# Projection matmuls of a hybrid decoder block issued in steps of three through the FoX, SSD and GLA stages, and the SSD convolution in two overlapping phases

## The chip, the cores and the metric

The kernel runs on one core of a Trainium2 chip. The metric is the device time of one execution in microseconds (us), lower is better. Engine names as in the profile: PE is TensorE (PEld its weight loads), DVE is VectorE, ACT is ScalarE, POOL is GpSimd, SP is SyncE, which here only issues DMAs.

## What is computed

One decoder layer over 1024 tokens of width 1024, batch 1, float32:

```
h = rms_norm(x);  p = h @ W_in          # 3352 columns, cut among four head groups
x += W_out @ concat[ FoX attention | Mamba-2 SSD | GLA | HGRN2 ]   # 256 wide each
x += cross_attention(rms_norm(x), rms_norm(mem))                   # 256 memory tokens
x += conv_glu_ffn(rms_norm(x))                                     # 2816 wide
```

FoX is causal softmax attention with 4 heads of 64 and a forget bias. SSD runs a causal convolution of width 4 with a SiLU over 512 channels, then a chunked scan in 8 chunks of 128 tokens. GLA and HGRN2 are chunked gated linear attentions. The memory's keys and values are `rms_norm(mem) @ xa_wkv`.

## The kernel before

**Projections.** Every large product is made of float32 numbers split in a high and a low part, so one 128-row contraction costs three matmuls (`split_matmuls`, lines 99 to 101). The input projection is cut in 27 items of 128 columns. An item has two halves of 512 tokens, and a half is 8 contraction blocks, thus 24 matmuls of 128x512 into one of two PSUM buffers (`mix_gb`). Here three matmuls of one contraction block are called a step: a half is 8 steps. For each item ACT writes the high part of the weights (line 432), DVE the low part (line 739), and ACT copies each finished half out of PSUM (line 444). The half m needs the low part of its item (semaphore `g_lo`) and half m-2 copied out (`g_ev`). After the input projection, 16 further items (`kv`) multiply the memory's rows with `xa_wkv`; each of them is 4 steps. SP loads each item two items ahead.

**Stages and order.** Each engine's program is written out by hand, stage after stage: normalise x, project; HGRN2; preparation of FoX; FoX; SSD; GLA; then another block (`tail_block`) with W_out, cross attention and feed-forward. While a stage's own work keeps DVE and ACT busy, TensorE is given projection work of the stage after it. How many halves go where is a table of counts that `spread` turns into ranges; all engines walk the same table, each doing its share of a half at that place:

```
_FX = spread(2 * S0, 2 * G0, [1] * 6 + [1 if n in (4, 9, 14, 20, 25, 30) else 0 for n in range(33)])
_SD = spread(2 * G0, 2 * N_ITEMS, [2, 2, 1, 1] + [1] * 6 + [0] * 2)
```

- Preparation of FoX: six rounds. In each, PE does two norm matmuls (line 1074), one half of projection, and transposes of v (line 1180); ACT squares (484), takes Ln (491) and Exp (493), and copies v; DVE multiplies (750). Then ACT and DVE gate HGRN2's output (tanh line 537; DVE 754, 755), and only then DVE begins FoX's logits (875).
- FoX: 33 bodies, 32 units (head pair, block of 128 queries, head). Body n on PE: scores of unit n+1 (1205), projection if the table has any (6 bodies), then `outputs(n-1)`: transposes of the probabilities (1219), a wait for ACT's copy of them (617), and their product with v (1227). DVE makes logits and probabilities (875 to 885), ACT the exponentials (606).
- SSD: the convolution takes 4 tiles of 128 channels. For each tile ACT starts with scale and bias (646), DVE adds three taps (908 twice, 910), ACT takes Tanh (649), DVE forms the product (913). PE does 6 halves meanwhile. Then 8 chunks: PE does a half (chunks 0 to 5), the inputs of the next chunk (1256, 1261, 1266), then the outputs (1292, 1294, 1297). A chunk's outputs wait for DVE's and ACT's work on the chunk, which waits for the outputs of the chunk before. ACT's memory statistics (467 to 472) and DVE's scaling (962) come in chunk 5, the transposes of the memory (1280) in chunks 6 and 7.
- Preparation of GLA: gates, norms of SSD's output, and a chain of exponentials and products (987 to 1009), with the `kv` items 0 to 10 on PE. Then 8 GLA tiles (1317 to 1349) with no projection, then items 11 to 15 among the last norms.

Of the kernel before, what the change touches and what calls it, by code (L numbers as in the profile page):

```python
# [156 lines left out]
FOX_PRE, FOX_UNIT = _FX[:6], _FX[6:]  # L157
_SD = spread(2 * G0, 2 * N_ITEMS, [2, 2, 1, 1] + [1] * 6 + [0] * 2)
SSD_CONV, SSD_CHUNK = _SD[:4], _SD[4:]


KV_ITEMS = 4 * KT // 2


MEM_STATS, MEM_TR = NT - 3, NT - 2


def mixers_block(nc, cst, a, SL, MX, HH, HL, x, FCW, FCB):
# [4 lines left out]
    with Phase(nc, "mix") as ph:  # L173
# [248 lines left out]
        def _(act):  # L422
# [156 lines left out]
            for j in range(6):  # L579
                rstd(2 * j)  # L580
                rstd(2 * j + 1)
                if j < 5:
                    squares(2 * j + 2)
                    squares(2 * j + 3)
                halves(*FOX_PRE[j])
# [36 lines left out]
            for n in range(len(FOX_UNITS) + 1):  # L622
# [8 lines left out]
                halves(*FOX_UNIT[n])  # L631
                fox_out(n - 1)
            copy_out(2 * G0)
# [6 lines left out]
            for t in range(4):  # L640
                halves(*SSD_CONV[t])
# [3 lines left out]
                y, th = mx(4 + t % 2), data(B + 6 + t % 2)  # L645
                act.activation(y, data(B + 2 + t), ACT.Identity, scale=CWS[:, t, 3:4], bias=CBS[:, t:t + 1])\
                   .then_inc(E("conv_in"), 1)
                act.wait_ge(E("conv_sum"), t + 1)
                act.activation(th, y, ACT.Tanh).then_inc(E("conv_th"), 1)
            for c in range(NT):  # L650
                halves(*SSD_CHUNK[c])
                if c == MEM_TR:
                    copy_out(2 * N_ITEMS)
# [4 lines left out]
                act.activation(EA, M[2][:], ACT.Exp).then_inc(E("s_ea"), 1)  # L658
                if c == MEM_STATS:
                    memory_stats()  # L660
                if c >= MEM_TR:
                    memory_hi(c - MEM_TR)

            act.wait_ge(E("s_upd"), NT)
            act.wait_ge(E("s_yev"), NT)
            kv(0, 1)
            for p in range(2):
                gate(2 + p, data(B + p), data(B + 6 + p))
            kv(1, 2)
# [8 lines left out]
            kv(2, 4)  # L678
            rstd(18)
            rstd(19)  # L680
            kv(4, 6)
# [5 lines left out]
            kv(6, 7)  # L687
            act.wait_ge(E("gl_cum"), 1)
            act.activation(data(B + 6), data(B + 7), ACT.Exp, scale=1.0 / 16).then_inc(E("gl_e1"), 1)
            kv(7, 8)  # L690
            act.wait_ge(E("gla_q"), 1)
            act.activation(data(B + 6), data(B + 7), ACT.Exp, scale=-1.0 / 16).then_inc(E("gl_e2"), 1)
            kv(8, 9)
            act.wait_ge(E("gl_te"), 1)
            act.activation(data(B + 7), data(B + 7), ACT.Exp, scale=1.0 / 16).then_inc(E("gl_e3"), 1)
            kv(9, 11)
# [9 lines left out]
            kv(11, 12)  # L706
# [9 lines left out]
            kv(12, 14)  # L716
            rstd(22)
            rstd(23)
            kv(14, 15)
# [7 lines left out]
        def _(dve):  # L727
# [126 lines left out]
            for j in range(6):  # L854
                norms(2 * j, 2 * j + 2)
                halves(*FOX_PRE[j])
# [30 lines left out]
            for n in range(33):  # L887
# [3 lines left out]
                halves(*FOX_UNIT[n])  # L891
                if n:
                    probabilities(n - 1)
                if n in (0, 16):
# [7 lines left out]
            for t in range(4):  # L902
                s = B + 2 + t
                y, th = mx(4 + t % 2), data(B + 6 + t % 2)
                halves(*SSD_CONV[t])
                dve.wait_ge(E("conv_in"), t + 1)
                for j in (2, 1):
# [3 lines left out]
                   .then_inc(E("conv_sum"), 1)  # L911
                dve.wait_ge(E("conv_th"), t + 1)
                dve.scalar_tensor_tensor(data(s), th, 1.0, y, ALU.add, ALU.mult).then_inc(E("conv_out"), 1)
            dve.wait_ge(E("conv_out"), 4)
            S = S_SSD
            for c in range(NT):
                sd = SCD[c % 2]
                halves(*SSD_CHUNK[c])
# [37 lines left out]
                dve.nop().then_inc(E("s_upd"), 1)  # L956
                if c == MEM_STATS:
# [7 lines left out]
                if c >= MEM_TR:  # L965
# [6 lines left out]
            kv(0, 1)  # L972
            gate(2, data(B), data(B + 6), mx(2))
            kv(1, 2)
            gate(3, data(B + 1), data(B + 7), mx(3))
            norms(16, 18)
            kv(2, 4)
# [3 lines left out]
            kv(4, 6)  # L981
# [12 lines left out]
            kv(6, 7)  # L994
# [4 lines left out]
            kv(7, 8)  # L999
# [7 lines left out]
            kv(8, 9)  # L1007
            dve.wait_ge(E("gl_e3"), 1)
            dve.tensor_tensor(k, k, u, ALU.mult).then_inc(E("gl_kend"), 1)
            kv(9, 11)  # L1010
# [20 lines left out]
            kv(11, 12)  # L1031
            norms(20, 22)
            kv(12, 14)
            norms(22, 24)
            kv(14, 15)
# [5 lines left out]
        def _(pe):  # L1041
            def halves(m0, m1):
                for m in range(m0, m1):
                    n, h = half_at(m)
                    if h == 0:
                        pe.wait_ge(E("g_lo"), n + 1)
                    if m >= 2:
                        pe.wait_ge(E("g_ev"), m - 1)
                    for k in range(KT):
                        mm = split_matmuls(pe, gb[m % 2][:], WH[:, n % PART, k, :], WL[:, n % PART, k, :],  # L1050
                                           half(HH[:, k, :], h), half(HL[:, k, :], h), k == 0, k == KT - 1)
                    mm.then_inc(E("g_mm"), 1)

            def kv(j0, j1):
                for j in range(j0, j1):
                    n, (c, kk) = N_ITEMS + j, divmod(j, KT // 2)
                    pe.wait_ge(E("g_lo"), n + 1)
                    if kk == 0:
                        pe.wait_ge(E("g_ev"), 2 * (N_ITEMS + c))
                    for t in range(2):  # L1060
                        tok = slice(t * P, (t + 1) * P)
                        for b in range(2):
                            k = 2 * kk + b
                            mm = split_matmuls(pe, gb[t][:], HH[:, k, tok], HL[:, k, tok], two_rows(WH, n % PART)[:, b, :],
# [1158 lines left out]
```

## Time and profile before

| what | value |
|---|---|
| median of 3 executions | 1868.43 us |
| the three executions | 1868.43, 2946.23, 1867.78 us |
| the profiled execution | 1867.99 us |
| its span in the trace | 1866.2 us |
| TensorE busy in the span | 1731.4 us (93%) |
| mean granted TensorE clock | 0.966 of full speed |

The span is what the trace covers; 1.8 us of the profiled execution lie outside it. Busy times of TensorE are modelled from pipelined matmuls and overlap one another, so the spacing of the starts is what a matmul costs.

### The profile page before, as it was taken

To read this page: it belongs to the slowest core of one execution; us is meant where nothing else is said; L and a number is where in the kernel's file an instruction comes from. 1 tells how busy PE (TensorE), PEld (TensorE's weight loads), DVE (VectorE), ACT (ScalarE), POOL (GpSimd) and SP (SyncE) were. 2 spreads that over 40 slices of the span, in tenths; PEclk is the share of its full clock that TensorE was granted. 3 is DMA by queue.
4 is the path that set the end of the run, shared out by engine and by line. 5 is a ranking of instruction groups with operands and counts; after the bars stand their busy time and mean duration, and the time that the engine had idled before them with its cause. 6 is when DMAs were issued, how large, how long until landed. Compare 5 with 4: busy or idle time off the path is not lost.

```text
span 1866.2 us, 20863 instructions
## 1 busy us (share of the span) xinstructions
PE 1731.4 (93%) x8076; PEld 1374.7 (74%) x8076; DVE 889.6 (48%) x1487; ACT 676.2 (36%) x1218; POOL 74.2 (4%) x119
## 2 busy tenths in 40 slices
PE   6999998988888769699999999999999999999997
PEld 5787665655567546587888888888888888888886
DVE  4315584453636656545334434555543355555332
ACT  5224103633452353634434322434432334344321
POOL 2000430000001002000000000000000000000000
PEclk8999998898999899899999999999999999999999
DMA  4122000000002021350001102333323333433232
GB/s 138 45 47 46 13 12 12 23 12 12 12 23 68 12 68 57 111 194 11 14 1 46 45 29 87 94 102 91 96 74 96 101 113 98 123 92 107 85 96 96
DMA packets 166922, 121.32 MB, mean 65 GB/s; under 512 B 23448, under 2 KB 140456, under 8 KB 166824
## 3 DMA queue, kind: packets, MB, share of 16 engines
q1 hardware_dynamic: 165496, 115.53, 20.8%
q10 hardware_dynamic: 1328, 4.46, 0.7%
q8 instruction: 65, 1.06, 0.2%
q14 instruction: 33, 0.27, 0.0%
HBM read 115.77 MB, written 4.19 MB: 64 GB/s over the span
## 4 chain that ended last, share of the span: by engine, by line
PE 57%; DVE 1%; ACT 0%; DMA 0%; issue 0%; DVEq 0%
PE tail_b L99 17%; PE tail_b L101 17%; PE tail_b L100 17%; PE tail_b L2065 2%; PE tail_b L2040 1%; PE tail_b L2029 0%; PE tail_b L2052 0%; PE tail_b L1977 0%; DVE tail_wl L1741 0%; DMA tail_wr<-in_w_out 0%; PE tail_b L2184 0%; PE tail_b L2100 0%; DVE tail_xs L1776 0%; ACT tail_xs L1576 0%; DVE XR L1904 0%
## 5 line engine op out<-in xcount | busy, mean ns | idle before, releaser
L1897 DVE TENSOR_TENSOR ff_wl<-ff_wr,ff_wh 128x512 fp32r<-128x512 f32 (+1 forms) x176 | 168.5, 958 | 329.9 <-ACT ff_wh L1684 329.9
L1684 ACT ACTIVATE ff_wh<-ff_wr 128x512 fp32r<-128x512 f32 (+1 forms) x176 | 148.7, 846 | 377.9 <-PE tail_b L101 377.9
L99 PE MATMUL tail_b<-HH,ff_wh 128*128 128x512 f32 x704 | 273.9, 389 | 0.0
L100 PE MATMUL tail_b<-HL,ff_wh 128*128 128x512 f32 x704 | 273.9, 389 | 0.0
L101 PE MATMUL tail_b<-HH,ff_wl 128*128 128x512 f32 x704 | 273.9, 389 | 0.0
L99 PE MATMUL mix_gb<-HH,mix_wh 128*128 128x512 f32 x432 | 178.3, 413 | 7.7 <-ACT slots L444 3.8
L100 PE MATMUL mix_gb<-HL,mix_wh 128*128 128x512 f32 x432 | 171.5, 397 | 0.0
L101 PE MATMUL mix_gb<-HH,mix_wl 128*128 128x512 f32 x432 | 170.8, 395 | 0.0
L99 PE MATMUL tail_b<-tail_wh,HH 128*128 128x512 f32 x384 | 153.9, 401 | 10.0 <-DVE tail_wl L1741 8.8
L100 PEld LDWEIGHTS tail_b<-HL,ff_wh 128*128 128x128 f32 x704 | 132.2, 188 | 27.7
L99 PEld LDWEIGHTS tail_b<-HH,ff_wh 128*128 128x128 f32 x704 | 132.2, 188 | 27.5
L101 PEld LDWEIGHTS tail_b<-HH,ff_wl 128*128 128x128 f32 x704 | 132.2, 188 | 27.1
L101 PE MATMUL tail_b<-tail_wh,HL 128*128 128x512 f32 x384 | 150.3, 391 | 0.0
L100 PE MATMUL tail_b<-tail_wl,HH 128*128 128x512 f32 x384 | 150.2, 391 | 0.0
L739 DVE TENSOR_TENSOR mix_wl<-mix_wr,mix_wh 128x1024 fp32r<-128x1024 f32 x43 | 53.6, 1247 | 113.9 <-ACT mix_wh L432 113.3
L99 PEld LDWEIGHTS mix_gb<-HH,mix_wh 128*128 128x128 f32 x432 | 83.5, 193 | 32.5 <-ACT slots L444 5.3
L99 PE MATMUL tail_b<-ff_wh,ff_aha 128*128 128x512 f32 x256 | 100.2, 392 | 0.0
L100 PE MATMUL tail_b<-ff_wl,ff_aha 128*128 128x512 f32 x256 | 99.7, 389 | 0.0
L100 PEld LDWEIGHTS mix_gb<-HL,mix_wh 128*128 128x128 f32 x432 | 83.4, 193 | 18.6 <-issue 1.7
L101 PEld LDWEIGHTS mix_gb<-HH,mix_wl 128*128 128x128 f32 x432 | 83.0, 192 | 17.9
L99 PEld LDWEIGHTS tail_b<-tail_wh,HH 128*128 128x128 f32 x384 | 72.6, 189 | 24.8 <-issue 11.0
L101 PEld LDWEIGHTS tail_b<-tail_wh,HL 128*128 128x128 f32 x384 | 72.4, 188 | 15.6
(311 smaller groups left out, 2661.7 us busy)
## 6 DMA issues: line engine op xcount, KB each, us to landing
ff_wr<-in_ffn_w_up SPq DMA_DIRECT2D x88, 512.0 KB, 3.7
ff_wr<-in_ffn_w_down SPq DMA_DIRECT2D x88, 256.0 KB, 2.8
mix_wr<-in_w_in SPq DMA_DIRECT2D x26, 512.0 KB, 3.7
mix_wr<-in_xa_wkv SPq DMA_DIRECT2D x16, 512.0 KB, 3.7
XR<-in_x SPq DMA_DIRECT2D x8, 512.0 KB, 6.4
tail_wr<-in_w_out SPq DMA_DIRECT2D x16, 256.0 KB, 5.2
XR<-in_x ACTq DMA_DIRECT2D x1, 4096.0 KB, 18.7
tail_wr<-in_xa_wq SPq DMA_DIRECT2D x16, 256.0 KB, 4.6
```

The lines of the kernel that those rows point to most:

```text
L99: pe.matmul(out, hi_w, hi_x, start=first, stop=False)
L100: pe.matmul(out, hi_w, lo_x, start=False, stop=False)
L101: return pe.matmul(out, lo_w, hi_x, start=False, stop=last)
L739: dve.tensor_tensor(WL[:, n % PART, :, :], WR[:, n % RAW, :, :], WH[:, n % PART, :, :], ALU.subtract)\
L1684: act.activation(part(FWH[m % FPART], m), part(FWR[m % FRAW], m), ACT.Copy).then_inc(w_hi, 1)
L1897: dve.tensor_tensor(part(FWL[m % FPART], m), part(FWR[m % FRAW], m), part(FWH[m % FPART], m), ALU.subtract)\
L2040: mm = pe.matmul(bank[3 + g][:, hh * N_MEM:(hh + 1) * N_MEM], QT[:, 2 * h + kk, :], ktr(2 * h + kk), start=(kk == 0), stop=(kk == 1))
L2065: mm = pe.matmul(bank3[6 + g][:, j, :], vv(m, d), PT[:, m, d // 2, :], start=(m == 0), stop=(m == 1))
```

## The change

No instruction of PE is added or taken away. The tables now count steps, and TensorE's `fill` issues a range of steps, which may begin or end inside a half. The other engines do their share of a half in the body in which it begins (`begun`). The steps go as follows (before in brackets):

- FoX preparation: 2 steps in each of 6 rounds (8).
- FoX: in bodies 1 to 31 except 16, 2 steps between the scores and the transposes (part A) and, unless n is a multiple of 4, one more between the transposes and the product with v (part B). Together 84 steps (48).
- SSD convolution: 9 steps for each of 4 tiles, 36 in all (48). On ACT the bias of two tiles is set first, and on DVE the taps of tile t+1 come ahead of the product of tile t.
- SSD chunks: 6 steps before and 6 after the next chunk's inputs, in chunks 0 to 4, 60 in all (48 in chunks 0 to 5). The memory's statistics come in chunk 4 and its transposes in chunks 5 and 6. The first `kv` item (4 steps) goes ahead of the outputs of chunk 7.
- GLA: 24 `kv` steps in the preparation (44), one step at each of two places in each of 8 tiles (0), then 4, 8 and 8 (the same).

```diff
+def FOX_FILL(n):
+    return (0, 0) if n in (0, 16) else (2, 1 if n % 4 else 0) if n < 32 else (0, 0)
...
-_FX = spread(2 * S0, 2 * G0, [1] * 6 + [1 if n in (4, 9, 14, 20, 25, 30) else 0 for n in range(33)])
-_SD = spread(2 * G0, 2 * N_ITEMS, [2, 2, 1, 1] + [1] * 6 + [0] * 2)
+def begun(span):
+    return -(-span[0] // KT), -(-span[1] // KT)
+_FX = spread(2 * S0 * KT, 2 * G0 * KT, [2] * 6 + [c for n in range(33) for c in FOX_FILL(n)])
+_SD = spread(2 * G0 * KT, 2 * N_ITEMS * KT, [9] * 4 + [c for n in range(NT) for c in ((6, 6) if n < 5 else (0, 0))])
+_KV = spread(0, KV_ITEMS * KV_STEPS, [4] + [4, 4, 4, 4, 4, 4] + [c for n in range(NT) for c in (1, 1)] + [4, 8, 8])
-MEM_STATS, MEM_TR = NT - 3, NT - 2
+MEM_STATS, MEM_TR = NT - 4, NT - 3
...
 # ACT, FoX body
-                halves(*FOX_UNIT[n])
                 fox_out(n - 1)
+                halves(*begun((FOX_A[n][0], FOX_B[n][1])))
...
 # ACT, convolution
+            conv_bias(0)
+            conv_bias(1)
+            for t in range(4):
+                halves(*begun(SSD_CONV[t]))
+                conv_tanh(t)
+                if t + 2 < 4:
+                    conv_bias(t + 2)
...
 # DVE, convolution
+            conv_taps(0)
+            for t in range(4):
+                halves(*begun(SSD_CONV[t]))
+                if t + 1 < 4:
+                    conv_taps(t + 1)
+                conv_gate(t)
...
 # PE
+            def fill(s0, s1):
+                for s in range(s0, s1):
+                    m, k = divmod(s, KT)
+                    n, h = half_at(m)
+                    if k == 0 and h == 0:
+                        pe.wait_ge(E("g_lo"), n + 1)
+                    if k == 0 and m >= 2:
+                        pe.wait_ge(E("g_ev"), m - 1)
+                    mm = split_matmuls(...)
+                    if k == KT - 1:
+                        mm.then_inc(E("g_mm"), 1)
...
-                halves(*FOX_UNIT[n])
-                outputs(n - 1)
+                fill(*FOX_A[n])
+                outputs(n - 1, FOX_B[n])
...
 # PE, SSD chunk c
-                halves(*SSD_CHUNK[c])
+                fill(*SSD_A[c])
...
                     ssd_inputs(c + 1)
+                fill(*SSD_B[c])
+                if c == NT - 1:
+                    pe.wait_ge(E("mem_lo"), 4)
+                    kv(*KV_SSD)
...
 # PE, GLA tile i
                 gla_states(i)
+                kv(*KV_A[i])
                 if i + 1 < NT:
                     gla_scores(i + 1)
+                kv(*KV_B[i])
                 gla_outputs(i)
```

TensorE in FoX, first half of the heads, around the unit with four blocks of keys, before (L1205 scores, L1219 transposes, L1227 product with v):

```order
L1205 MATMUL mix_m<-XR 128x512
L1205 MATMUL mix_m<-XR 128x128
L1219 MATMUL mix_m<-ident,slots 128x128 x4
L1227 MATMUL mix_m<-mix_scratch,slots 64x128 x4
L1205 MATMUL mix_m<-XR 128x512
```

and in the changed kernel, where L1251, L1265 and L1274 are those three lines:

```order
L1251 MATMUL mix_m<-XR 128x512
L1251 MATMUL mix_m<-XR 128x128
L99 MATMUL mix_gb<-HH,mix_wh 128x512
L100 MATMUL mix_gb<-HL,mix_wh 128x512
L101 MATMUL mix_gb<-HH,mix_wl 128x512
L99 MATMUL mix_gb<-HH,mix_wh 128x512
L100 MATMUL mix_gb<-HL,mix_wh 128x512
L101 MATMUL mix_gb<-HH,mix_wl 128x512
L1265 MATMUL mix_m<-ident,slots 128x128 x4
L99 MATMUL mix_gb<-HH,mix_wh 128x512
L100 MATMUL mix_gb<-HL,mix_wh 128x512
L101 MATMUL mix_gb<-HH,mix_wl 128x512
```

The row L1274 follows. Two steps now stand ahead of the transposes and one behind them; before, this body had none.

ACT at the start of the SSD convolution, before (L432 weights, L444 copy out, L646 bias, L649 Tanh):

```order
L432 ACTIVATE mix_wh<-mix_wr 128x1024
L444 ACTIVATE slots<-mix_gb 128x512
L646 ACTIVATE XR<-slots,mix_cbs,mix_cws 128x1024
L649 ACT_TABLE_LOAD
L649 ACTIVATE slots<-XR 128x1024
L444 ACTIVATE slots<-mix_gb 128x512
```

and in the changed kernel (L456, L468, L670 and L675 in the same roles):

```order
L670 ACTIVATE XR<-slots,mix_cbs,mix_cws 128x1024 x2
L456 ACTIVATE mix_wh<-mix_wr 128x1024
L468 ACTIVATE slots<-mix_gb 128x512
L675 ACT_TABLE_LOAD
L675 ACTIVATE slots<-XR 128x1024
L670 ACTIVATE XR<-slots,mix_cbs,mix_cws 128x1024
```

The bias of the first tile no longer stands behind a copy that waits for TensorE's first half.

## Rows read from the trace of the kernel before

**Rows 1.** The page: the span, and TensorE's granted clock in 40 slices.
```profile
span 1866.2 us, 20863 instructions
...
PEclk8999998898999899899999999999999999999999
```

**Rows 2.** Busy per stage: stretch, length, PE, PEld, DVE, ACT, POOL, granted clock, DMA share, GB/s.
```profile
307.10:357.60 50.50, 50.46 (x192) 35.22 (x192) 16.85 (x19) 33.87 (x57) 0.00 (x0) 0.96 0.12 32
357.60:437.60 80.00, 67.76 (x337) 45.67 (x336) 43.19 (x91) 32.12 (x77) 0.00 (x0) 0.94 0.05 14
...
533.80:572.90 39.10, 32.96 (x145) 26.97 (x145) 23.91 (x19) 16.99 (x19) 0.52 (x1) 0.97 0.16 41
572.90:631.40 58.50, 57.15 (x343) 46.89 (x343) 34.33 (x83) 14.89 (x25) 5.85 (x16) 0.96 0.16 55
631.40:658.40 27.00, 14.33 (x70) 9.53 (x69) 17.13 (x41) 6.65 (x15) 0.00 (x0) 0.68 0.00 1
658.40:713.30 54.90, 39.03 (x142) 28.15 (x141) 34.08 (x33) 29.11 (x35) 2.91 (x2) 0.91 0.29 95
713.30:746.70 33.40, 32.24 (x202) 19.28 (x200) 20.22 (x42) 7.55 (x16) 8.70 (x7) 0.97 0.06 18
```

**Rows 3.** Timeline ahead of FoX: start, length, engine, line, operation, last wait in brackets.
```profile
324.37 1.88 PE L1074 MATMUL mix_m<-slots,mix_bo 128*128 128x512 f32 x4
...
325.43 0.69 ACT L491 ACTIVATE slots<-mix_m,eps 128x512 f32<-128x512 f32 x1 [0.42 <-PE mix_m L1074]
...
327.92 1.14 ACT L484 ACTIVATE slots<-XR 128x512 f32<-128x512 f32 x2
...
347.90 0.69 ACT L491 ACTIVATE slots<-mix_m,eps 128x512 f32<-128x512 f32 x1 [2.12 <-PE mix_m L1074]
...
358.58 0.35 DVE L875 SCALAR_TENSOR_TENSOR slots<-mix_m,mix_st,slots 128x128 f32<-128x128 f32 x1 [0.32 <-PE mix_m L1205]
```

**Rows 4.** TensorE's timeline, one FoX body near 415 us.
```profile
411.69 0.87 PE L1219 MATMUL mix_m<-ident,slots 128*128 128x128 f32 x6
413.12 1.50 PE L1227 MATMUL mix_m<-mix_scratch,slots 128*64 128x128 f32 x12 [0.56 <-ACT mix_scratch L617]
...
416.46 0.77 PE L1219 MATMUL mix_m<-ident,slots 128*128 128x128 f32 x5
```

**Rows 5.** TensorE's timeline, projection matmuls in FoX body 20.
```profile
456.77 0.63 PE L99 MATMUL mix_gb<-HH,mix_wh 128*128 128x512 f32 x1
457.20 0.63 PE L100 MATMUL mix_gb<-HL,mix_wh 128*128 128x512 f32 x1
...
457.92 0.40 PE L99 MATMUL mix_gb<-HH,mix_wh 128*128 128x512 f32 x1
...
460.68 0.39 PE L99 MATMUL mix_gb<-HH,mix_wh 128*128 128x512 f32 x1
```

**Rows 6.** Timeline, third tile of the SSD convolution.
```profile
559.89 2.60 DVE L908 SCALAR_TENSOR_TENSOR XR<-slots,mix_cws,XR 128x1024 f32<-128x1024 f32 x2
...
563.84 1.06 ACT L649 ACTIVATE slots<-XR 128x1024 f32<-128x1024 f32 x1 [3.99 <-DVE XR L910]
...
564.93 1.22 DVE L913 SCALAR_TENSOR_TENSOR slots<-slots,XR 128x1024 f32<-128x1024 f32 x1 [1.13 <-ACT slots L649]
```

**Rows 7.** TensorE's timeline, first output matmuls of SSD chunks 5, 6 and 7.
```profile
629.91 0.45 PE L1292 MATMUL mix_m<-XR,slots 128*64 128x128 f32 x4
...
642.16 0.70 PE L1292 MATMUL mix_m<-XR,slots 128*64 128x128 f32 x4
...
652.51 0.70 PE L1292 MATMUL mix_m<-XR,slots 128*64 128x128 f32 x4 [3.73 <-DVE XR L937]
```

**Rows 8.** Timeline from the SSD norms to the first GLA tile.
```profile
680.24 0.69 ACT L491 ACTIVATE slots<-mix_m,eps 128x512 f32<-128x512 f32 x1 [4.13 <-PE mix_m L1074]
...
689.28 0.74 DVE L987 TENSOR_SCALAR slots<-mix_m,mix_bg 128x512 f32<-128x512 f32 x1
...
713.30 0.49 PE L1317 MATMUL mix_m<-ident,slots 128*128 128x128 f32 x3
```

More of the change, by code:

```diff
@@ L584, in _ @@
                     squares(2 * j + 3)
-                halves(*FOX_PRE[j])
+                halves(*begun(FOX_PRE[j]))
                 for i in (2 * j, 2 * j + 1):
@@ L639, in _, with conv_bias @@
             act.wait_ge(E("mixed"), 2)
-            for t in range(4):
-                halves(*SSD_CONV[t])
+            conv_y = lambda t: mx(4 + t % 2)
+            def conv_bias(t):
                 act.wait_ge(E("half_w"), 1)
@@ L855, in _ @@
                 norms(2 * j, 2 * j + 2)
-                halves(*FOX_PRE[j])
+                halves(*begun(FOX_PRE[j]))
             for p in range(2):
@@ L890, in _ @@
                     logits(n)
-                halves(*FOX_UNIT[n])
                 if n:
                     probabilities(n - 1)
+                halves(*begun((FOX_A[n][0], FOX_B[n][1])))
                 if n in (0, 16):
@@ L899, in _, with conv_taps @@
             dve.nop().then_inc(E("mixed"), 1)
[L902 to L905, printed above, removed]
+            def conv_taps(t):
+                s, y = B + 2 + t, mx(4 + t % 2)
                 dve.wait_ge(E("conv_in"), t + 1)
@@ L917, in _ @@
                 sd = SCD[c % 2]
-                halves(*SSD_CHUNK[c])
                 dve.wait_ge(E("s_tr"), c + 1)
@@ L956, in _ @@
                 dve.nop().then_inc(E("s_upd"), 1)
+                halves(*begun((SSD_A[c][0], SSD_B[c][1])))
                 if c == MEM_STATS:
@@ L1054, in kv @@
[L1054 to L1064, printed above, removed]
-                                               two_rows(WL, n % PART)[:, b, :], k == 0, k == KT - 1)
+            def fill(s0, s1):
[6 more added lines that the diff above has]
+                        pe.wait_ge(E("g_ev"), m - 1)
+                    mm = split_matmuls(pe, gb[m % 2][:], WH[:, n % PART, k, :], WL[:, n % PART, k, :],
+                                       half(HH[:, k, :], h), half(HL[:, k, :], h), k == 0, k == KT - 1)
+                    if k == KT - 1:
+                        mm.then_inc(E("g_mm"), 1)
@@ new lines, in halves, with kv @@
+            def halves(m0, m1):
+                fill(KT * m0, KT * m1)
+            def kv(u0, u1):
+                for u in range(u0, u1):
+                    j, (t, b) = u // KV_STEPS, divmod(u % KV_STEPS, 2)
+                    n, (c, kk) = N_ITEMS + j, divmod(j, KT // 2)
+                    k, tok = 2 * kk + b, slice(t * P, (t + 1) * P)
+                    if t == 0 and b == 0:
+                        pe.wait_ge(E("g_lo"), n + 1)
+                        if kk == 0:
+                            pe.wait_ge(E("g_ev"), 2 * (N_ITEMS + c))
+                    mm = split_matmuls(pe, gb[t][:], HH[:, k, tok], HL[:, k, tok], two_rows(WH, n % PART)[:, b, :],
+                                       two_rows(WL, n % PART)[:, b, :], k == 0, k == KT - 1)
+                    if b == 1:
@@ L1172, in _ @@
                 norms(2 * j, 2 * j + 2)
-                halves(*FOX_PRE[j])
+                fill(*FOX_PRE[j])
                 for i in (2 * j, 2 * j + 1):
@@ L1206, in scores, with outputs @@
                               start=True, stop=True).then_inc(E("sc_mm"), 1)
-            def outputs(n):
+            def outputs(n, between):
                 hp, i, hh = FOX_UNITS[n]
@@ L1220, in outputs @@
                     last.then_inc(E("p_tr"), 1)
+                fill(*between)
                 if n >= 1:
@@ L1242, in _ @@
                     scores(n + 1)
-                halves(*FOX_UNIT[n])
-                outputs(n - 1)
+                fill(*FOX_A[n])
+                outputs(n - 1, FOX_B[n])
             norms(12, 16)
@@ L1249, in _ @@
             for t in range(4):
-                halves(*SSD_CONV[t])
+                fill(*SSD_CONV[t])
             pe.wait_ge(E("conv_out"), 4)
@@ L1300, in _ @@
                 pe.matmul(M[h][:], WG2[:], half(data(SMALL), h), start=True, stop=True).then_inc(E("gate_mm"), 1)
-            pe.wait_ge(E("mem_lo"), 4)
-            kv(0, 2)
+            kv(*KV_PREP[0])
             norms(16, 18)
-            kv(2, 4)
+            kv(*KV_PREP[1])
             norms(18, 20)
-            kv(4, 6)
-            kv(6, 11)
+            for part in KV_PREP[2:]:
+                kv(*part)
             pe.wait_ge(E("gl_kin"), 1)
```

91 lines of the change are left out of this document (45 added, 46 removed).

## The prediction

> **What bounds the kernel now.** I read the page first. TensorE is the engine to fill: its granted clock is near full almost everywhere, and the slices that are not lie in the first half of the span [rows 1]. So the question is by stage, and the busy time by stretch comes next [rows 2]. From 307 to 747 us TensorE's modelled busy time leaves gaps: 12.2 us of 80.0 in the first half of FoX, 12.7 of 27.0 in SSD's last chunks, 15.9 of 54.9 ahead of GLA. In the preparation of FoX (50.5 us) and in SSD chunks 0 to 5 (58.5 us) it is nearly full. No work is added or removed, so the change can gain only what TensorE now waits, and it moves work from places that are full to places that wait. The timeline tells the price of a step. Its starts are 0.23 us apart at full clock (12 matmuls from 457.92 to 460.68) and 0.43 us at the low one [rows 5]: a step of three costs 0.69 us, a half 5.5 us.
>
> The time is worked out as a walk down TensorE's program, stage by stage, each term measured from the end of the stage before it.
>
> **Preparation of FoX.** Four steps of every eight, and two more, leave each round, 36 in all, or 24.8 us of work. What is late next is ACT. A round now takes 7.49 us (the first Ln of round 3 is at 325.43, that of the sixth at 347.90, three rounds). ACT's two pairs of Ln and Exp take 2.49 (325.43 to 327.92), the next square 0.57 (half of 1.14), about 0.1 until the norm matmul starts, and its Ln follows 1.06 after that (324.37 to 325.43) [rows 3]. That is a loop of 4.2 us, while TensorE has 1.7 of norms, 0.4 of transposes and 1.4 of steps, 3.5 us. I take 4.25 us. The first round, which keeps its weight conversion, saves 2.9; four more save 3.25 each, 13.0. One copy out of PSUM (0.6) leaves ACT's way between the last Exp and the tanh of the gates. DVE's gates then still end last before the first logits at 358.58 [rows 3]. Term: -16.5 us.
>
> **FoX bodies.** 84 steps instead of 48. Part B goes where TensorE waits for ACT's copy: six transposes start at 411.69 and the product with v at 413.12; at 0.11 us each (twelve matmuls of that width last 1.50) the transposes are over at 412.34, so 0.78 us are a wait [rows 4]. A step there costs 0.69 and about 0.14 for the turn from it, so 0.05 us net; up to 0.26 where a unit has seven blocks of keys, nothing where it has four. I take 0.8 us per half of the heads for the nine B steps in bodies 5 to 15. Part A has no wait to hide in once a unit has four blocks: a body of 4.77 us (411.69 to 416.46) is work of TensorE [rows 4], and two steps cost 1.38 and a turn, 1.5 us. In the first bodies of a half it is hidden in part: there the transposes wait for DVE, and matmuls run at 0.43 [rows 5].
> Per half: taken out, three halves of 5.5 and 0.15 (one of them partly at the low clock, 1.6 us more), 18.6 us. Put in, eleven bodies with A at 1.5 (16.5), B 0.8, bodies 1 to 4 together 2.4: 19.7. Term for both: +2.1 us, for 24.8 us of work taken on. If no B step were hidden, 24 of them would add 16 us more; that is the upper bound of this term. If A hid as well, it would be some 10 us less; that is the lower.
>
> **SSD convolution.** It takes 39.1 us [rows 2], of which 48 steps are 33. The DVE rows give its own chain: three taps 3.95 us (559.89 to 563.84), tanh 1.09, product 1.22 [rows 6]. Now the first bias doesn't wait for half 42, and a tile's tanh runs beside the next one's taps. Followed through: taps of tile 0 end 5.2 us after the start, weights' low part 6.4, taps 1 at 10.3, product 0 at 11.6. Then a loop stays: bias 2 waits for product 0, and the ACT part of the next item comes before tanh 1, so taps 2 start at 15.7 and end at 19.6; product 1 at 20.9, bias and taps 3 at 26.0, product 2, the last low part and product 3 at 29.8 us. TensorE is done with 36 steps at 24.8, so DVE ends last. Term: 29.8 instead of 39.0, -9.2 us.
>
> **SSD chunks with steps.** A chunk has 12 steps (8.2 us) and 3.6 us of its own work and turns, 11.8; 8 steps took 8.8 to 9.9. From the first chunk's steps to the first output matmul of the last chunk that has steps it was 54.1 us, six chunks (it is 629.91 there [rows 7]); five chunks now give 4 times 11.75, 10.3 up to the outputs, and 0.6 for one wait for low weights in chunk 2: 57.9. What waits is less than before, since ten microseconds of TensorE's work cover the 7 to 8 of DVE and ACT. Term: +3.8 us.
>
> **SSD chunks without.** Here the change gives back. Chunks without steps are bound by the chain through DVE and ACT: 12.25 us with the memory's scaling (629.91 to 642.16) and 10.35 with its low part (to 652.51), at a clock of 0.68 [rows 2, 7]. Before there were two of them, now three: 12.25, 10.35 and 10.35. Besides, ACT's statistics now stand behind the copy of half 53, which TensorE finishes just before its outputs; DVE waits 1.4 us for them. The `kv` item in chunk 7 (2.7 us) hides in this wait. Term: 34.35 instead of 22.6, +11.8 us.
>
> **GLA.** From the outputs of chunk 7 (652.51) to the first tile it is 60.8 us now (713.30 [rows 7, 8]). With 24 steps instead of 44 the chain of ACT and DVE is bare. The second pair of norms waits for two items (Ln at 680.24); with one it comes at 673.4, and DVE's first GLA operation, now at 689.28 behind two low parts [rows 8], at 677. From there the chain is the same to the last product (at 696), and the seventh item ends at about 697.9. Term: -15.4 us. The tiles are TensorE's: 32.2 of 33.4 us busy [rows 2]. Sixteen steps put in add 11.0, their turns 2, one wait for the copies of `gb` 0.8; the last tile hides 1.8. Term: +12.0 us.
>
> **The sum.** -16.5 + 2.1 - 9.2 + 3.8 + 11.8 - 15.4 + 12.0 = -11.4 us. Against the profiled execution of 1867.99 us (a span of 1866.2 [rows 1] and 1.8 outside it) that is 1856.6; the median of the runs shown is 0.4 higher. I forecast 1857 us, 0.6% less, and so no change that a measurement of this kernel, which tells about 2%, can be sure to see.
>
> **Rival 1: full clock and better hiding (1846 us).** The low stretches of the clock cost matmuls double [rows 5], and steps in nearly every FoX body leave TensorE no long wait. If the clock then stays full at the start of both halves and in the chunks without steps (3 us), and part A hides where I charge it 1.5 us, in a third of 22 bodies (8 us), it is 11 us less. For it: the small bodies at 0.43 us per matmul. Against it: in large bodies TensorE has no wait ahead of the transposes.
>
> **Rival 2: the spread costs what it hides (1866 us).** Steps are begun and ended inside halves, so copies out and low weights can be late in a body. If each of the ten step places of the SSD chunks and every fourth of 54 in FoX loses 0.4 us (4 + 5 us), the gain is 2. For it: ACT now does its share after the exponentials of the chunk. Against it: by the walk above, a copy is two bodies early in FoX.
>
> **Rival 3, slower: TensorE thinned out until its clock drops (1874 us).** In the preparation of FoX it now has 3.5 us of work in 4.25, in that of GLA 24 steps in 45 us. Behind the small units of FoX the trace shows matmuls 0.43 us apart instead of 0.23, the lower of the two levels, 1.2 instead of 2.4 GHz [rows 5], and in SSD's bare chunks a mean of 0.68 of the clock [rows 2]. If it falls in the preparation, a round's work is 7 us instead of 3.5 and passes ACT's 4.25; the round is back near 7.3. It decides from the round in which TensorE's work passes 4.25 us. Price: of the 15.9 us 13 are lost, 2 in the first bodies, and 2 ahead of GLA: +17, 1874. Against it: between 380 and 440 us waits of 0.8 us in each body leave nearly the whole clock (0.94 over that half of FoX with its start [rows 2]).
> The Trainium skill's page "TensorE: Matmul & The Clock Gate", section "What's actually happening", states that the slow clock is the default state and that only activity lifts it, which speaks against spreading work thinly. By that rule the outcome is this rival's 1874 us if the thinned rounds lose the clock, and 1857 us if they keep it; no row here shows rounds of this kind.
>
> **How the numbers follow.** Forecast 0.5 (1851 to 1864 of its own), rival 1 0.22, rival 2 0.16, rival 3 0.12. Bounds: the FoX term reaches from -10 to +16 around its value, the SSD terms some 6 either way, and these seldom agree. A range of 1834 to 1873 leaves out the far part of rival 1 and most of rival 3. Faster by over 2% (below 1831) needs more than rival 1's gain twice over: 0.06. Slower by over 2% needs 37 us: 0.01. Within 2%: 0.93.
>
> **What would show it.** In the profile after: ACT's Ln (L515) in the preparation 4.25 us apart and the first logits near 342; a step between transposes and product (L1265, L1274) with no wait behind it; the convolution 30 us; three SSD output groups over 10 us apart, not two; the first GLA tile 45 us after chunk 7's outputs and tiles of 5.3 us. It would be wrong if rounds stay at 7 us, if bodies with part A grow by less than 1 us, or if the bare chunks take under 9 us.

## The result, and the profile after

The changed kernel takes 1882.97 us (median of 20 executions, 1881.44 to 1891.2), the kernel before 1868.5 us (20 executions, one of them 2946 us and left out of the ratio). The ratio is 1.0078, 95% interval 1.0062 to 1.0094. So the change costs 14.5 us (11.6 to 17.6), under 1% but clear of the spread, where 11 us less was forecast; 1883 lies outside the range of 1834 to 1873. The profiled execution took 1890.98 us, 8 us over the median. Of that, 4.7 us are in HGRN2's stage, ahead of everything that the change touches, at a granted clock of 0.70 in a stretch where the kernel before had 0.93; the stages below are therefore each counted from the end of the one before.

The page of the changed kernel, to be laid beside [rows 1]:

```profile
span 1889.0 us, 20864 instructions
...
PEclk8999988899999888999999999999999999999999
```

The instructions are the same in number but for one. After the first slice the clock is under 0.9 in slices 6 to 8 (236 to 378 us) and 14 to 16 (614 to 756 us), before in 7, 8, 10, 14 and 17 [rows 1]; most of FoX lies between them, so the page alone doesn't place the loss. The windows by stage, columns as in [rows 2] (stretch, length, PE, PEld, DVE, ACT, POOL, granted clock, DMA share, GB/s):

```profile
311.80:345.00 33.20, 28.02 (x84) 15.33 (x84) 13.54 (x16) 29.19 (x51) 0.00 (x0) 0.92 0.06 17
345.00:444.60 99.60, 85.02 (x391) 57.09 (x390) 44.97 (x93) 34.39 (x80) 0.00 (x0) 0.90 0.06 16
444.60:538.20 93.60, 85.52 (x398) 56.44 (x398) 42.42 (x90) 35.29 (x83) 0.00 (x0) 0.95 0.05 12
538.20:579.10 40.90, 31.15 (x120) 21.84 (x118) 26.27 (x23) 24.43 (x31) 0.52 (x1) 0.96 0.10 27
579.10:648.00 68.90, 62.91 (x331) 50.31 (x331) 28.73 (x67) 12.15 (x20) 4.96 (x16) 0.95 0.16 54
648.00:684.00 36.00, 22.32 (x117) 16.13 (x117) 20.90 (x48) 10.91 (x19) 0.00 (x0) 0.72 0.00 0
684.00:726.40 42.40, 26.66 (x100) 18.32 (x97) 30.85 (x35) 23.96 (x29) 1.99 (x2) 0.84 0.22 74
726.40:771.40 45.00, 44.09 (x248) 28.12 (x247) 24.32 (x46) 12.47 (x22) 8.67 (x7) 0.96 0.18 60
```

They are, in order: preparation of FoX, FoX's first and second half, convolution (with the norms ahead of it), SSD chunks with steps, chunks without, preparation of GLA, GLA tiles. FoX takes 193.2 us. The same count made of each trace by the first and last matmuls of the stages gives this account; the predicted terms stand beside it.

| stage | before, us | after, us | difference | predicted |
|---|---|---|---|---|
| preparation of FoX | 50.5 | 33.2 | -17.3 | -16.5 |
| FoX | 164.4 | 193.2 | **+28.8** | +2.1 |
| convolution, with norms | 50.8 | 40.8 | -10.0 | -9.2 |
| SSD chunks | 79.6 | 104.5 | **+24.9** | +15.6 |
| preparation of GLA | 60.8 | 42.8 | -18.0 | -15.4 |
| GLA tiles | 33.2 | 45.1 | +11.9 | +12.0 |
| after them, to the first transposes of the next block | 92.4 | 90.2 | -2.2 | 0 |

The sum is +18.1, and 4.7 ahead of the first row make up the 22.8 us by which the two spans differ. Two terms failed. For FoX the waits are asked first, on DVE, in 345 to 540 us (waiting line, releaser: us in total, times, longest), and below it the same wait in the kernel before, in 357 to 522 us:

```profile
DVE mix_wl L773 <- ACT mix_wh L456: 40.5, 5, 10.1
```
```profile
DVE mix_wl L739 <- ACT mix_wh L432: 9.8, 3, 3.6
```

DVE writes the low part of an item's weights (line 773) from the high part that ACT writes (line 456). It waits up to 10.1 us for it, five times in FoX; before, up to 3.6 us, three times. Two things moved: on ACT the share of the projection went behind the outputs (line 644), as the diff of the change shows, and on DVE, which that diff leaves out, from ahead of the probabilities to behind them. The timeline of the changed kernel around the third of the five waits (start, length, engine, line, operation, idle time and releaser):

```profile
427.30 1.74 PE L1274 MATMUL mix_m<-mix_scratch,slots 128*64 128x128 f32 x14
...
429.07 0.27 ACT L644 ACTIVATE XR<-mix_m 64x128 f32<-64x128 f32 x1 [1.73 <-PE mix_m L1274]
...
429.37 0.60 ACT L468 ACTIVATE slots<-mix_gb 128x512 f32<-128x512 f32 x1
...
429.86 1.05 ACT L456 ACTIVATE mix_wh<-mix_wr 128x1024 fp32r<-128x1024 f32 x1
...
430.95 1.22 DVE L773 TENSOR_TENSOR mix_wl<-mix_wr,mix_wh 128x1024 fp32r<-128x1024 f32 x1 [10.12 <-ACT mix_wh L456]
432.09 1.40 DVE L909 SCALAR_TENSOR_TENSOR slots<-mix_m,mix_st,slots 128x512 f32<-128x512 f32 x2
...
435.18 0.75 DVE L919 TENSOR_SCALAR slots<-slots,mix_rin 128x1024 f32<-128x1024 f32 x1
435.98 1.57 PEld L1265 LDWEIGHTS mix_m<-ident,slots 128*128 128x128 f32 x8 [5.79 <-DVE slots L919]
435.99 1.97 PE L1265 MATMUL mix_m<-ident,slots 128*128 128x128 f32 x8 [5.36 <-DVE slots L919]
...
437.61 0.78 PE L99 MATMUL mix_gb<-HH,mix_wh 128*128 128x512 f32 x1
437.99 0.60 ACT L641 ACTIVATE mix_scratch<-mix_m 128x512 f32<-128x512 f32 x1 [0.26 <-PE mix_m L1265]
438.18 0.63 PE L100 MATMUL mix_gb<-HL,mix_wh 128*128 128x512 f32 x1
...
438.61 0.63 PE L101 MATMUL mix_gb<-HH,mix_wl 128*128 128x512 f32 x1
```

Read it upwards from TensorE's 5.36 us. Its transposes wait for DVE's probabilities (919). These wait behind DVE's logits (909) of the next unit, which start at 432.09, right behind the low part. The low part stood ready in DVE's program for 10.1 us and waited for ACT's 456. ACT's 456 and the copy 468 stand in ACT's program behind line 644, which scales and writes out the unit before, and 644 waits for TensorE's product (1274). So DVE, which is normally a body or two ahead of TensorE, is held until TensorE has finished the body before; its lead is gone, and TensorE pays. Behind the wait matmuls start 0.57 and 0.43 us apart (437.61, 438.18, 438.61), where at full clock it is 0.23 [rows 5]. TensorE's own waits in 345 to 540 us add up to this, and those of the kernel before in 357 to 522 us to what stands in the second block:

```profile
PE mix_m L1265 <- DVE slots L919: 12.4, 5, 5.4
PE mix_m L1251 <- DVE slots L909: 5.6, 2, 2.8
PE mix_m L1274 <- ACT mix_scratch L641: 4.5, 8, 0.8
```
```profile
PE mix_m L1227 <- ACT mix_scratch L617: 19.8, 32, 1.3
PE mix_m L1219 <- DVE slots L885: 4.4, 2, 2.4
```

The waits for DVE are 18.0 us over five items; before, they were 4.4 us, two times. The waits for ACT's copy fell from 19.8 to 4.5 us, as part B was meant to do. So 15.3 us of waits went and 13.6 us of others came: in sum the 36 further steps were hardly hidden.

### The profile page after: what moved, and what is told of

It reads as the page before. It is cut to its first block, busy times and chain, and to the rows that moved or that the text cites. A ratio compares the mean times of both kernels' runs of the same rounds, so it can differ in the third digit from the quotient of the medians.

```text
span 1889.0 us, 20864 instructions
## 1 busy us (share of the span) xinstructions
PE 1747.8 (93%) x8076; PEld 1380.4 (73%) x8076; DVE 887.8 (47%) x1487; ACT 675.2 (36%) x1218; POOL 72.4 (4%) x119
## 4 chain that ended last, share of the span: by engine, by line
PE 56%; DVE 1%; ACT 0%; DMA 0%; issue 0%; DVEq 0%
PE tail_b L99 17%; PE tail_b L101 17%; PE tail_b L100 17%; PE tail_b L2115 2%; PE tail_b L2090 1%; PE tail_b L2079 0%; PE tail_b L2102 0%; PE tail_b L2027 0%; DVE tail_wl L1791 0%; DMA tail_wr<-in_w_out 0%; PE tail_b L2150 0%; PE tail_b L2234 0%; DVE tail_xs L1826 0%; ACT tail_xs L1626 0%; DVE XR L1954 0%
## 5 line engine op out<-in xcount | busy, mean ns | idle before, releaser
L99 PE MATMUL mix_gb<-HH,mix_wh 128*128 128x512 f32 x432 | 186.1, 431 | 7.9 <-ACT slots L468 4.0
L101 PEld LDWEIGHTS tail_b<-tail_wh,HL 128*128 128x128 f32 x384 | 72.5, 189 | 15.6
```

Source lines behind the costliest of these rows:

```text
L99: pe.matmul(out, hi_w, hi_x, start=first, stop=False)
L101: return pe.matmul(out, lo_w, hi_x, start=False, stop=last)
```

## The experiments

Ten runs, each timed beside the kernel before. All but the seventh are edits of the changed kernel. In diffs, `share(n)` stands for `halves(*begun((FOX_A[n][0], FOX_B[n][1])))`, ACT's or DVE's part of the projection in body n.

**1. The share where it stood before.**

```diff
 ACT   fox_exp(n)
-      fox_out(n - 1)
       share(n)
+      fox_out(n - 1)
 DVE   logits(n)
+      share(n)
       probabilities(n - 1)
-      share(n)
```

> The changed kernel, with ACT's and DVE's share of a half (copy out, high part, low part) back at its old place in each FoX body: on ACT ahead of the copies of the unit's outputs, on DVE between logits and probabilities. Theory A (in the changed kernel this share stands behind the outputs, so DVE's next logits wait for a low part that waits for a high part that waits for TensorE's outputs; some 3 to 6 us at each of 6 items, and a low clock after it): the stall is cut but not gone, since the copy now waits for a half that ended only in part A of the same body, and the probabilities stand behind it, about 3 us per item. FoX, 193 us in the changed kernel and 164 before, comes to 180 to 186, the time to 1870 to 1877. Rival B (steps in small pieces cost turns and clock, wherever the share stands): FoX stays at 190 to 193, the time at 1880 to 1883.

Measured: 1882.17 us, ratio 1.0049 (1.0020 to 1.0078); FoX 188.5 us. Only 4.7 us of FoX came back, less than theory A said and more than rival B: this run alone decides nothing. TensorE's waits for the probabilities are no less than in the changed kernel (12.4 us):

```profile
PE mix_m L1265 <- DVE slots L919: 13.3, 7, 2.9
```

The share is now ahead of the outputs on ACT, but on DVE it sits ahead of probabilities that TensorE needs next. The copy that theory A blamed is a small part: in FoX, ACT waited 6.2 us in all for a half to end. Experiment 9 differs from this run in DVE's place alone and takes 165.2 us in FoX, so DVE's place is the cause here.

**2. The share a body later on both engines.**

```diff
 ACT   fox_exp(n)
+      share(n - 1)
       fox_out(n - 1)
-      share(n)
 DVE   logits(n)
+      if n and n != 16: share(n - 1)
       probabilities(n - 1)
-      share(n)
```

> As e1_fox_share_first, but the share of a half that begins in body n is done in body n+1, where the half before it has long ended. Theory A: no engine waits for it any more; FoX comes to the 166 to 169 us of the prediction's walk and the time to 1857 to 1862, the first that is below the kernel before. Rival B: FoX 190 us and 1880 or more.

Measured: 1869.87 us, ratio 0.9999 (0.9966 to 1.0033); FoX 178.3 us, both well above what was expected (1857 to 1862, and 166 to 169). 14.9 of the 28.8 us are back, with no change to TensorE's own program. That the companion engines' order is a cause was now shown; that it was the whole of it was not. The trace still had TensorE waiting for line 919 seven times, up to 3.7 us and 13.0 in all, since on DVE the share again stood ahead of the probabilities.

**3. No steps between transposes and product (part B).** On top of experiment 2:

```diff
-    return (0, 0) if n in (0, 16) else (2, 1 if n % 4 else 0) if n < 32 else (0, 0)
+    return (0, 0) if n in (0, 16) else (3 if n % 4 else 2, 0) if n < 32 else (0, 0)
```

> e2_fox_share_later with the 24 steps of part B moved ahead of the transposes, into part A (3, 0 in place of 2, 1). If the step between transposes and product hides in the wait for ACT's copy, as the prediction has it, it loses 24 times 0.6 to 0.7 us: 14 to 17 us more than e2, 1872 to 1876. If TensorE pays for a step there as elsewhere, it is within 3 us of e2.

Measured: 1882.44 us, ratio 1.0038 (1.0000 to 1.0075); FoX 191.8 us, 13.5 more than experiment 2. TensorE's waits in 300 to 540 us, here (first row) and in experiment 2 (second):

```profile
PE mix_m L1275 <- ACT mix_scratch L641: 17.5, 31, 0.8
```
```profile
PE mix_m L1275 <- ACT mix_scratch L641: 4.5, 8, 0.8
```

A wait for ACT's copy is in 31 bodies without part B and in 8 with it, 13.0 us more. Moving 24 steps costs 13.5 / 24 = 0.56 us each by the two profiles, 0.52 by the medians (12.6 us), of the 0.69 that a step takes: part B hides as forecast (0.05 to 0.26 net by the prediction, 0.13 to 0.17 here), and it was not the loss. The two figures are not clean of the clock: of the 13.5 us, 5.1 are longer busy time of TensorE at a granted clock of 0.96 for 0.98.

**4. Eight and four steps in an SSD chunk instead of six and six.** On top of experiment 2:

```diff
-... ((6, 6) if n < 5 else (0, 0))])
+... ((8, 4) if n < 5 else (0, 0))])
```

> e2_fox_share_later with 8 and 4 steps in SSD chunks 0 to 4 in place of 6 and 6. In the changed kernel TensorE waits 0.8 to 2.1 us in four of the five chunks ahead of line 1308, the inputs that overwrite what ACT's exponential (line 689) still reads. Theory C (this wait is the SSD term's miss, as 6 steps are shorter than the chain of ACT and DVE): two more steps cover it, the SSD chunks get 5 to 7 us shorter, 1851 to 1856. Rival D (the chunks are longer for low weights that come late, or for the clock): within 2 us of e2.

Measured: 1865.43 us, ratio 0.9956 (0.9921 to 0.9990), 4.4 us under experiment 2, and the SSD chunks 98.8 us instead of 104.1, as theory C said; the 1851 to 1856 us was missed because it took experiment 2 at its own forecast. TensorE's waits for the exponential (line 689) ahead of the transposes of the next chunk's inputs, in 520 to 680 us, in experiment 2 and then here:

```profile
PE mix_m L1309 <- ACT XR L689: 9.4, 6, 1.9
```
```profile
PE mix_m L1309 <- ACT XR L689: 4.1, 4, 1.6
```

**5. DVE's share, a body later, behind the probabilities.** On top of experiment 4:

```diff
 DVE   logits(n)
-      if n and n != 16: share(n - 1)
       probabilities(n - 1)
+      if n and n != 16: share(n - 1)
```

> e4_ssd_8_and_4 with one move in FoX: DVE makes the low part behind the probabilities again (as the changed kernel does), while ACT's copy and high part stay a body late and ahead of the output copies (as in e2 and e4). In e2 TensorE still waited 2.0 to 4.0 us at five of the six items, because the probabilities stood behind a low part that stood behind ACT's exponential, copy and high part. Theory A: both places matter, and now neither the probabilities nor the next logits wait: FoX falls from 179 to 167 to 170 us, the time from 1865.4 to 1853 to 1857. Rival B (what is left in FoX is turns and clock): FoX stays at 176 or more, 1863 to 1866.

Measured: 1852.16 us, ratio 0.9898 (0.9843 to 0.9954, four executions of this kernel); FoX 166.1 us, so 12.9 more come back (179.0 in the profile of experiment 4). TensorE now waits for the probabilities 2.1 us instead of 13 (experiment 2). Both places matter, ACT's and DVE's.

**6. Steps in six chunks instead of five.** On top of experiment 5, with the memory's statistics and transposes one chunk later and the `kv` item of the last chunk behind the chunks:

```diff
-... ((8, 4) if n < 5 else (0, 0))])
+... ((8, 2) if n < 6 else (0, 0))])
-MEM_STATS, MEM_TR = NT - 4, NT - 3
+MEM_STATS, MEM_TR = NT - 3, NT - 2
```

> e5 with the 60 steps of the SSD chunks spread over six chunks (8 before and 2 behind the next inputs) instead of five, the memory's statistics and transposes a chunk later, as in the kernel before, and the first kv item behind the chunks. Theory: a chunk without steps costs 10 to 14 us for 3.6 us of TensorE's work, so a third one of them is a loss of 6 to 8 us; giving it steps brings the chunk stage from 98.8 to 89 to 92 us, the first kv item gives 2.7 back later; 1849 to 1853. Rival: the chain of the filled chunks is then the bound and the gain is under 2 us.

Measured: 1843.36 us (four executions), ratio 0.9848 (0.9798 to 0.9897), 6 us under the expected range; the chunks take 89.5 us instead of 98.6, within it. That is nearly the whole length of the last bare chunk in the changed kernel (9.7 us, below).

**7. The kernel before, with the convolution in two phases and nothing else.** ACT issues bias 0 and 1 first, then per tile its share of the projection, tanh t, bias t+2; DVE taps 0, then per tile its share, taps t+1, product t.

> The kernel before with one part of the change alone, the convolution in two overlapping phases on ACT and DVE; TensorE's order is as before, with 48 steps in it. By the walk of the prediction ACT and DVE need 30 us, but TensorE's 48 steps need 33, so TensorE becomes the bound: 39.1 us fall to 33.5 to 35, the time by 4 to 5.5 us, 1863 to 1865. Rival (the two phases only help with fewer steps): no change.

Measured: 1863.36 us, ratio 0.9967 (0.9923 to 1.0010). 5.3 us less, as forecast, though the interval reaches 1 and no difference is proven. Its profiled execution was one of the two of ten that took 1883 us; in it the convolution with its norms is 4.0 us shorter than before, while FoX, whose code is that of before, took 176.3 us instead of 164.4. This number is the reason for not reading 12 us out of one trace of one stage.

**8. The change with preparation and bodies of FoX as before.** The table of FoX again gives whole halves to six bodies, and ACT's and DVE's share stands as in experiment 1.

```diff
-... [2] * 6 + [c for n in range(33) for c in FOX_FILL(n)])
+... [8] * 6 + [c for n in range(33) for c in
+               ((8, 0) if n in (4, 9, 14, 20, 25, 30) else (0, 0))])
```

> The changed kernel with FoX and its preparation as before, in counts and places; convolution, SSD chunks and GLA as changed. By the stages of the profiles the changed kernel gains 17.3 us in the preparation and loses 28.8 in FoX, so this comes 11 to 12 us under it, at 1870 to 1872, and the rest of the change (convolution -10, chunks +25, GLA -8) is 2 to 6 us slower than the kernel before by itself. Rival (FoX's loss is not its own, but the state of the clock or weights it inherits): FoX would not return to 164 us.

Measured: 1871.81 us, ratio 1.0009 (0.9986 to 1.0032); FoX is back at 164.5 us. The rest of the change does nothing that could be measured; the prediction's five terms for it add up to +3.0, and the median is 3.1 us up. The FoX part of the change, preparation included, costs 11.2 us (1882.97 less 1871.81) where the prediction had -14.4: nearly the whole of the miss of 26 us.

**9. Two lines of ACT swapped, nothing else.**

```diff
                 if n < 32:
                     fox_exp(n)
-                fox_out(n - 1)
                 halves(*begun((FOX_A[n][0], FOX_B[n][1])))
+                fox_out(n - 1)
```

> The changed kernel with two lines of ACT's FoX body swapped and nothing else: the copy out and high part of a half ahead of fox_out, in the body in which the half begins; DVE keeps its low part behind the probabilities. If the loss in FoX is that ACT's high part waits for TensorE's outputs, this alone takes FoX from 193 to 167 to 172 us, as the half ACT waits for ends in part A, ahead of those outputs; the time 1856 to 1862. If the share has to be a body late, as in e5, FoX stays above 178 and the time above 1866.

Measured: 1859.17 us (1858.68 to 1860.24, four executions), ratio 0.9895 (0.9816 to 0.9975): 23.8 us under the changed kernel, and 10.7 under the kernel before, whose median beside it was 1869.9. FoX takes 165.2 us. Its windows, preparation and FoX:

```profile
307.20:340.40 33.20, 27.78 (x84) 15.03 (x84) 13.57 (x16) 29.16 (x51) 0.00 (x0) 0.94 0.06 17
340.40:505.60 165.20, 157.23 (x788) 106.24 (x788) 87.41 (x183) 69.36 (x163) 0.00 (x0) 1.00 0.06 17
```

DVE's wait for the high part in the same kernel, and one place of the timeline that answers to 429.07 above:

```profile
DVE mix_wl L773 <- ACT mix_wh L456: 20.8, 5, 5.3
```
```profile
406.92 1.14 ACT L630 ACTIVATE slots<-slots,mix_nm 128x1024 f32<-128x1024 f32 x1
...
408.05 0.58 ACT L468 ACTIVATE slots<-mix_gb 128x512 f32<-128x512 f32 x1
408.52 1.05 ACT L456 ACTIVATE mix_wh<-mix_wr 128x1024 fp32r<-128x1024 f32 x1
...
409.61 1.23 DVE L773 TENSOR_TENSOR mix_wl<-mix_wr,mix_wh 128x1024 fp32r<-128x1024 f32 x1 [4.46 <-ACT mix_wh L456]
...
410.75 1.41 DVE L909 SCALAR_TENSOR_TENSOR slots<-mix_m,mix_st,slots 128x512 f32<-128x512 f32 x2
```

The copy and the high part now follow the exponentials (630) directly. DVE still waits 5 us, but is still ahead of TensorE: TensorE's waits for the probabilities (919) fall from 12.4 us to 2.1, those for the logits (909), 5.6 us, to none.

```profile
PE mix_m L1265 <- DVE slots L919: 2.1, 2, 1.7
```

By the windows, TensorE is busy for 157.2 of 165.2 us, at a clock of 1.00; in the changed kernel for 85.0 and 85.5 of 193.2. So of the 28.0 us between them 14.7 are waits (22.7 less 8.0) and 13.3 longer matmuls at a lower clock.

They stand at the items. Counted from one body's scores (1251) to the next one's, bodies without an item take the same in both kernels: the one ahead of the rows below takes 5.14 us in each, the one behind them 5.57 and 5.56. The body of the second item takes 10.18 us in the changed kernel and 5.58 here:

```profile
387.84 1.12 PE L1251 MATMUL mix_m<-XR 64*128 64x512 f32 x2
...
398.02 1.34 PE L1251 MATMUL mix_m<-XR 64*128 64x512 f32 x3
```
```profile
376.78 1.55 PE L1251 MATMUL mix_m<-XR 64*128 64x512 f32 x4
...
382.36 1.55 PE L1251 MATMUL mix_m<-XR 64*128 64x512 f32 x4
```

With the bodies of experiments 1 and 9 the two places come apart. ACT's share behind its outputs and DVE's behind the probabilities (the changed kernel) gives 193.2 us in FoX; both ahead (experiment 1) 188.5; ACT's ahead and DVE's behind (experiment 9) 165.2. Neither order on one engine is enough by itself.

**10. Experiments 9 and 6 together.** The six chunks of experiment 6 on the kernel of experiment 9.

> e6_six_chunks with the two swapped lines in place of the share a body late. As simple as e9 and, if e9's first expectation holds, within 3 us of e6: 1842 to 1847.

Measured: 1844.06 us (four executions), ratio 0.9822 (0.9753 to 0.9891); FoX 165.2 us, chunks 87.8. It is equal to experiment 6, so behind the two swapped lines the lagged share of experiment 5 has nothing left to give. Both beat the kernel before, by 1.5 and 1.8% by the ratios and by 1.4% by the medians, and the changed one by 2.1% by the medians.

## Why the prediction was wrong

**Preparation of FoX: right.** -17.3 for -16.5. The loop of ACT that was to be late next is what is seen, with Ln (line 515) every 4.33 us for a predicted 4.25:

```profile
319.36 0.69 ACT L515 ACTIVATE slots<-mix_m,eps 128x512 f32<-128x512 f32 x1
...
323.69 0.69 ACT L515 ACTIVATE slots<-mix_m,eps 128x512 f32<-128x512 f32 x1 [0.15 <-PE mix_m L1120]
...
328.02 0.69 ACT L515 ACTIVATE slots<-mix_m,eps 128x512 f32<-128x512 f32 x1 [0.15 <-PE mix_m L1120]
```

The first logits came at 346.86 us, 35 us after the first norm matmul; it was 51.4 before.

**FoX bodies: this is the step that failed.** The term priced what TensorE does, step by step, and of ACT and DVE it asked only whether their results are there when TensorE's projection wants them. The sentence on rival 2, "by the walk above, a copy is two bodies early in FoX", asks only that. The copy was indeed early enough for TensorE, which never waited for it in FoX, and it did not matter. What I did not price is what stands behind the share on its own engine. ACT's share had moved behind `fox_out`, an instruction that waits for TensorE's product; DVE's low part waits for it, and DVE's logits wait behind the low part. A chain PE, ACT, DVE, PE within one body replaced a lead of a body or two. The prediction had nothing for this; the runs show 28.0 us in FoX. Experiment 9 is the proof, since it moves only ACT's line and takes 23.8 us off. With it the FoX term is +0.8 (165.2 less 164.4) against the +2.1 predicted. The prices of the steps were right: nine bodies with part A (378.18 us on in the kernel before, 357.53 us on in experiment 9, the cost of one half, 5.65 us, taken out) grow by 1.43 to 1.64 us each, for 1.5 and the little for part B that were forecast, and experiment 3 gives part B apart. The working of part B has a slip that did no harm: twelve matmuls in 1.50 us [rows 4] are 0.125 us each and not 0.11, which makes the wait 0.68 us and not 0.78. The new place of ACT's share stood in the diff; a walk down ACT and DVE for one body with an item in it would have shown the loop.

That experiment 9 comes out at 1859.2 us, so near the 1857 forecast, is in part luck: in the changed kernel's stages the SSD term is 9.3 us over its forecast, and the five others beside FoX are together 6.5 us under theirs.

**Convolution: right.** -10.0 for -9.2. Experiment 7 shows the two parts of the term apart. The new order alone gives 5.3 us by the medians (not proven) and 4.0 in the stage of its profile, as TensorE's 48 steps (33 us of 39 [rows 2]) are in the way; the rest comes with 36 steps.

**SSD chunks with steps: failed in size.** From the first steps to the outputs of the last of these chunks it was 66.6 us (581.42 to 647.99) for 57.9. "Ten microseconds of TensorE's work cover the 7 to 8 of DVE and ACT" counted a chunk's work as one block. But the steps come in two groups, and the inputs of the next chunk stand between them: the transposes (1308) wait for ACT's exponential (689), which has only the first six steps (4.1 us) as cover. The changed kernel's timeline:

```profile
624.36 0.49 PE L1303 MATMUL mix_m<-ident,slots 128*128 128x128 f32 x3
...
626.04 0.58 ACT L689 ACTIVATE XR<-mix_m 128x512 f32<-128x512 f32 x1
...
626.68 1.37 PE L1308 MATMUL mix_m<-slots,ident 128*128 128x128 f32 x8 [1.83 <-ACT XR L689]
...
628.34 0.99 PE L99 MATMUL mix_gb<-HH,mix_wh 128*128 128x512 f32 x1
629.13 0.63 PE L100 MATMUL mix_gb<-HL,mix_wh 128*128 128x512 f32 x1
```

A wait of 1.83 us, and here too slower matmuls behind it. Over the kernel these waits are 9.0 us, six times. Experiment 4 gives 5.3 us of the 8.7 back by two more steps of cover; what the other 3.4 are was not tried. The diff of the change also leaves out that in each chunk DVE's share of the projection, like ACT's, moved from the first place to behind the scan's own work; no run moves it back.

**SSD chunks without: right in the sum.** TensorE's first output matmuls of chunks 4 to 7 in the changed kernel, beside [rows 7]:

```profile
647.99 0.45 PE L1343 MATMUL mix_m<-XR,slots 128*64 128x128 f32 x4
...
661.78 0.70 PE L1343 MATMUL mix_m<-XR,slots 128*64 128x128 f32 x4
...
673.92 0.70 PE L1343 MATMUL mix_m<-XR,slots 128*64 128x128 f32 x4
...
683.59 0.45 PE L1343 MATMUL mix_m<-XR,slots 128*64 128x128 f32 x4
```

The three chunks take 13.8, 12.1 and 9.7 us, 35.6 for the 34.35 predicted; one by one they are up to 1.8 us off their terms. Experiment 6, by which the third of them gets steps again, is 8.8 us faster than experiment 5.

**GLA: right.** Preparation -18.0 for -15.4, 2.6 us better than forecast, and tiles +11.9 for +12.0.

**The rivals.** Rival 1's clock was right where FoX ran without the loop (1.00 in experiment 9, against 0.93 over the same bodies before), but its 8 us of hidden part A did not come, as the bodies that grow by 1.43 us and more show. Rival 2 had the kind of cause, companion work late in a body, at 0.4 us a place; it is 18 us at five items, 3.6 each. Rival 3 said where the clock would fall, and that did not cost what it said: the thinned rounds kept 0.92 (before 0.96), and their 4.33 us. In the preparation of GLA the clock did fall, to 0.84 from 0.91 [rows 2], and the stage was still shorter than forecast. It was low again in the FoX bodies behind the waits, and in the bare chunks it was 0.72, no lower than before.

**What stays open.** Whether the lower clock in FoX has its cause in these waits was not tried apart from them: experiment 9 took both away. Experiment 7's profiled execution shows 176.3 us in FoX with the old order and no such waits, so the clock falls there without them too. Nor does it follow the sum of the waits: with the same steps in FoX, experiment 2 has 17.6 us without a matmul and 160.7 us of busy time, experiment 1 18.0 and 170.6, and experiment 3 26.0 and 165.8. And the profile of the changed kernel is of an execution 8 us over the median, of which 4.7 lie ahead of FoX; so 28.0 us is what one pair of profiles shows, 23.8 what the medians do.

## What to carry to other kernels

When work is spread over a pipeline, walk the program of every engine that does a share of it, not only of the one that is to be filled: ask of each share what it stands behind, and what stands behind it. A share belongs ahead of the instruction that waits for the filled engine's result (ACT's outputs here), and behind the work that this engine needs next (DVE's probabilities). Two lines of ACT's program were worth 24 us here, more than the 11 us that the whole change was forecast to give. Where fill is cut in two, each part must cover the chain that ends at its own consumer, so count the cover group by group.

## What the runs showed of the hardware

One program, run again and again on one chip, is not always granted the same clock. FoX with the code of the kernel before has 24.3 us without a matmul both in the profile of the kernel before and in that of experiment 7, but TensorE is busy for 140.2 us at a granted clock of 0.93 in the one and for 152.0 us at 0.85 in the other: 11.9 us for the clock alone. In HGRN2, at 237 to 262 us, the changed kernel was granted 0.70 where the kernel before had 0.93. Experiment 7's ten executions are eight at 1860 to 1865 us with a mean clock of 0.963 to 0.966, and two at 1883 us with 0.952; the changed kernel's twenty are 17 at 1881.4 to 1886.0 us with 0.964 to 0.969, and three at 1891 us with 0.960. So one profile can show a loss of 5 to 12 us in a stage that nobody touched, and a table of stages is to be read beside the median of many executions and a second profile.
